# Transposing the normalised tiles by a DMA on ScalarE's queue instead of by TensorE, in the middle tiles of a hybrid decoder layer

## What is computed

```python
def rmsnorm(x, g):
    y = x32 * rsqrt(mean(x32 * x32) + EPS) * g
...
p = einsum('btd,dc->btc', rmsnorm(x, norm1), w_in)       # u | q | k | v | o | gates
x = x + mixer_output(pool_mix(u), mlstm(q, k, v, gates), o)   # ends in @ w_out
a = square(relu(rmsnorm(x, norm2) @ w_up))
x = x + a @ w_down
y = rmsnorm(x, norm_f)
```

## Time and profile before

| | |
|---|---|
| median of 3 runs | 804.48 us (803.3 to 806.3) |
| profiled execution | 802.35 us, span of its slowest core 801.2 us |
| spans of the eight cores | 791.9 to 801.2 us |
| busy, share of the span | TensorE 95%, VectorE 54%, ScalarE 45%, GpSimd 20% |

### The profile page before, as it was taken

How to read it: one execution, slowest core, us unless ns; L and a number is a source line. 1 busy time by engine, 2 the same in 40 slices (tenths; PEclk the granted TensorE clock), 3 DMA queues, 4 the chain that set the end, 5 groups by cost and what they waited for, 6 DMA issues and landing times.

```text
span 801.2 us, 16676 instructions; the slowest of 8 cores (791.9 to 801.2 us)
## 1 busy us (share of the span) xinstructions
PE 761.0 (95%) x6707; PEld 532.0 (66%) x6707; DVE 432.9 (54%) x955; ACT 364.3 (45%) x871; POOL 160.9 (20%) x243
## 2 busy tenths in 40 slices
PE   2799899989999999999999899999999999999996
PEld 1678677858787789788789687878544444444443
DVE  1755886766886957786847765422233342421212
ACT  4465685854777564777664664422110010101102
POOL 7622430433303330202220300100011111100000
PEclk9789999999999999999999999999999999999999
DMA  8999995243444341334121989891666455453511
GB/s 151 202 184 179 185 188 112 72 94 81 53 108 124 82 107 54 67 105 107 54 81 60 158 189 244 173 220 62 203 214 241 176 217 215 148 193 124 180 54 53
DMA packets 35860, 110.43 MB, mean 138 GB/s; under 512 B 3431, under 2 KB 6871, under 8 KB 31798
## 3 DMA queue, kind: packets, MB, share of 16 engines
q1 hardware_dynamic: 21150, 63.31, 26.0%
q0 software_dynamic: 9648, 29.20, 22.7%
q10 hardware_dynamic: 4984, 16.86, 5.5%
HBM read 96.41 MB, written 39.64 MB: 170 GB/s over the span
## 4 chain that ended last, share of the span: by engine, by line
PE 81%; DVE 9%; DMA 5%; ACT 2%; issue 1%; POOL 1%; DVEq 0%; ACTq 0%; POOLq 0%; SPq 0%
PE B L428 79%; DMA wk<-w_in 2%; PE B L431 2%; DVE zt L437 2%; DMA aTd<-ast 1%; DMA C0b<-sC 1%; DVE ast L434 1%; DVE xt L434 1%; DVE mixh L437 1%; DVE rows L441 0%; DVE cols L434 0%; DVE rows L684 0%; POOL Wa L448 0%; ACT Dt L425 0%; DVE wsm L441 0%
## 5 line engine op out<-in xcount | busy, mean ns | idle before, releaser
L428 PE MATMUL B<-xn2T,wup 128*128 128x256 bf16 (+1 forms) x2304 | 248.7, 265 | 1.8 <-ACT rr L425 1.5
L428 PEld LDWEIGHTS B<-xn2T,wup 128*128 128x128 bf16 x2304 | 204.4, 98 | 27.7 <-ACT rr L425 2.0
L428 PE MATMUL B<-wdn,aTl 128*128 128x512 bf16 (+1 forms) x952 | 211.4, 379 | 0.0
L428 PEld LDWEIGHTS B<-wdn,aTl 128*128 128x128 bf16 (+1 forms) x952 | 93.1, 99 | 110.0
L434 DVE TENSOR_TENSOR xt<-xt,B 128x512 f32<-128x512 f32 (+1 forms) x68 | 46.5, 684 | 170.7 <-PE B L428 170.6
L434 DVE TENSOR_TENSOR ast<-rr 128x512 bf16<-128x512 f32 x132 | 95.6, 725 | 76.6 <-ACT rr L425 47.7
L425 ACT ACTIVATE rr<-B 128x512 f32<-128x512 f32 x132 | 78.1, 592 | 88.6 <-PE B L428 72.2
L425 ACT ACTIVATE junk<-xt 128x1024 bf16<-128x1024 f32 (+2 forms) x18 | 18.2, 1010 | 203.2 <-DVE xt L434 203.2
L428 PE MATMUL B<-w_out_sb,mixT 128*128 128x512 bf16 (+1 forms) x272 | 62.8, 379 | 0.0
L425 ACT ACTIVATE xn<-xt 128x1024 bf16<-128x1024 f32 (+2 forms) x34 | 35.7, 1050 | 33.6 <-DVE xt L434 23.3
L448 POOL TENSOR_TENSOR kz<-ktm,wsm 64x512 bf16<-64x512 bf16 x16 | 16.3, 1034 | 167.5 <-PE B L428 151.3
(11 more groups left out here) (202 smaller groups left out, 951.9 us busy)
## 6 DMA issues: line engine op xcount, KB each, us to landing
aTd<-ast SPq DMA_DIRECT2D x32, 512.0 KB, 4.7
aTl<-aTd SPq DMA_DIRECT2D x16, 1024.0 KB, 6.4
wup<-w_up POOLq DMA_DIRECT2D x8, 1024.0 KB, 38.4
x2d<-xt SPq DMA_DIRECT2D x16, 512.0 KB, 3.8
xt<-x2d SPq DMA_DIRECT2D x16, 512.0 KB, 3.4
yp<-xt ACTq DMA_DIRECT2D x15, 512.0 KB, 3.5
wdn<-w_down POOLq DMA_DIRECT2D x7, 1024.0 KB, 13.0
xt<-xp SPq DMA_DIRECT2D x12, 512.0 KB, 5.3
```

The costliest lines, as they stand in the source:

```text
L428: return lambda: nc.tensor.matmul(out, lhsT=lhsT, rhs=rhs, start=start, stop=stop)
```

## The change

In `pre` from tile 6 on, and in `tail` where `pos` is 6 to 14, `trT` is replaced by `XPOSE`: one transposing DMA, issued by ScalarE, that reads `xn` (128x1024, bfloat16, 256 KB) and writes `xnT` or the half of `xn2T` directly. The multiplication by the norm weights then reads and writes that tile in place in SBUF, where it used to read the PSUM bank. That is 11 tiles in `pre` and 9 in `tail`, so 20 times eight transposes leave TensorE. The planner is given 1.2 us of ScalarE for each such issue and 400,000 bytes for its transfer, and it makes a new order for all engines from there on.

```diff
--- before.py
+++ after.py
@@ -21,6 +21,7 @@
 UPV = 1800
 PRE, FRONT, MID, TAIL, POOLP, OGP = -50, -50, 30, -150, 40, 60
 NBC = 5
+TX0, TX1 = 6, 14
 LOG = None
 
 
@@ -277,7 +278,7 @@
                     hold[self.kinds[v]].add(v)
             if o.chan is not None:
                 q = 'sw' if o.eng == 'pool' else 'hw'
-                free[o.eng] = o.start + (1.0 if q == 'sw' else 0.3 if o.eng == 'act' else 0.4)
+                free[o.eng] = o.start + (1.0 if q == 'sw' else o.cost if o.cost > 1.0 else 0.3 if o.eng == 'act' else 0.4)
                 r = self.SW_RATE if q == 'sw' else self.HW_BUSY if band['sw'] > free[o.eng] + 1.0 else self.HW_RATE
                 b = max(free[o.eng] + 0.6, band[q]) + o.nbytes / r
                 if r == self.HW_BUSY:
@@ -430,6 +431,9 @@
         def tr(out, in_, identity):
             return lambda: nc.tensor.transpose(out=out, in_=in_, identity=identity)
 
+        def XPOSE(prio, out, in_, R, W, chan):
+            pl.add('act', [lambda: nc.scalar.dma_start_transpose(out=out, in_=in_)], R, W, 1.2, prio, chan, 400e3, 512)
+
         def vtt(out, in0, in1, op):
             return lambda: nc.vector.tensor_tensor(out=out, in0=in0, in1=in1, op=op)
 
@@ -847,9 +851,13 @@
             xk = 'xnT%d' % ix(pos); X = xnT[ix(pos)]
             xs_ = pos % NX
             norm(pr, xt[xs_][:], 'xt%d' % xs_, st[s2], 'st%d' % s2, 128)
-            T = trT(pr, 128)
-            V(pr, vtt(X[:], Bb[T].rearrange("p (k t) -> p k t", k=8), gcol1.unsqueeze(2).to_broadcast([128, 8, 128]), ALU.mult),
-              [bk(T), 'gvec'], [xk], 1.2)
+            if pos < TX0:
+                T = trT(pr, 128)
+                V(pr, vtt(X[:], Bb[T].rearrange("p (k t) -> p k t", k=8), gcol1.unsqueeze(2).to_broadcast([128, 8, 128]), ALU.mult),
+                  [bk(T), 'gvec'], [xk], 1.2)
+            else:
+                XPOSE(pr, X[:], xn[:], ['xn'], [xk], 'tx%d' % ix(pos))
+                V(pr, vtt(X[:], X[:], gcol1.unsqueeze(2).to_broadcast([128, 8, 128]), ALU.mult), [xk, 'gvec'], [xk], 1.2)
 
         def front(pos):
             i = pos - 1
@@ -1014,11 +1022,16 @@
             DMA(pr, 'sp', x2d[128 * i:128 * i + n, :], x_[r_, :], [xk], ['x2d%d' % i], 'x2s%d' % xs_, 512e3)
             sk = 'st%d' % (2 + pos % 2)
             norm(pr, x_[r_, :], xk, st[2 + pos % 2], sk, n)
-            T = trT(pr, n)
             gs, half = (0, 0) if sp_ else ((i // 2) % 2, i % 2)
             xnk = 'xn2T%d%d' % (gs, half)
-            V(pr, vtt(xn2T[gs][:, :, half * 128:half * 128 + n], Bb[T].rearrange("p (k t) -> p k t", k=8)[:, :, r_],
-                      gcol2.unsqueeze(2).to_broadcast([128, 8, n]), ALU.mult), [bk(T), 'gvec'], [xnk], 1.2)
+            X2 = xn2T[gs][:, :, half * 128:half * 128 + n]
+            gB = gcol2.unsqueeze(2).to_broadcast([128, 8, n])
+            if sp_ or not TX0 <= pos <= TX1:
+                T = trT(pr, n)
+                V(pr, vtt(X2, Bb[T].rearrange("p (k t) -> p k t", k=8)[:, :, r_], gB, ALU.mult), [bk(T), 'gvec'], [xnk], 1.2)
+            else:
+                XPOSE(pr, X2, xn[:], ['xn'], [xnk], 'ty%d%d' % (gs, half))
+                V(pr, vtt(X2, X2, gB, ALU.mult), [xnk, 'gvec'], [xnk], 1.2)
 
         for gs in range(2):
             for half in range(2):
```

## The result

The changed kernel takes 806.38 us (median of 20 runs) against 803.89 us for the kernel before on the same chip. The ratio is **1.0039, 95% interval 1.0021 to 1.0057**. It is slower by 0.4%, where 0.8% faster was forecast: the time lies inside the range that was given, on the wrong side of the kernel before.

The account below looks back on a forecast made before the run. TensorE's work was taken to bound the kernel, without gaps in tiles 6 to 16. 802.35 - 9.0 + 2.5 = 795.9 us, plus 2.1 to the median: 798.0 us, 0.8% faster; range 793.5 to 814 us.

Parts of the forecast that it names:

- What leaves TensorE: Tiles 6 to 16: twenty groups of eight transposes at 0.45 us leave TensorE, all on the path, -9.0 us.
- What VectorE gains or loses: Norm-weight multiplication: 1.22 us from PSUM, taken as 1.22 again from SBUF, so 0 us.
- What the issue costs ScalarE: Twenty DMA issues at up to 1.36 us each, covered by ScalarE's idle time and a second bank: 0 us.
- the sign of being wrong that the prediction named: On ScalarE's queue: the forecast is wrong if issues of the transposing DMA are over 2.3 us.
- the first rival: ScalarE eats the gain: 0.3 to 0.5 us behind each of 20 issues, 800.5 to 808 us, chance 0.2.
- What the landing costs: Next norm and multiplication wait for DMAs landing in 5.2 us: 0.5 us at five places, +2.5 us.
- the 15 us that the prediction named: Wrong if ScalarE's waits for `xn`, or VectorE's for `xnT` and `xn2T`, add up to over 15 us.
- the second rival: Late landings stop ScalarE at the next norm in fourteen places; 817 us at 7.9 us landings, chance 0.18.
- the third: Each DMA transposes its blocks one after another, landing far over every cover: 877 us, chance 0.04.
- What comes late at the end: Last `w_down` load before `up` ends: cover shrinks from 25 us to some 16, so 0 us.

Follow-up runs that it names:

- e8: The changed kernel's order on every engine, with the 20 transposing DMAs issued by SyncE instead of ScalarE: 803.8 us, 1.0012 of the kernel before.
- the two moves: Changed kernel, first `down` matmuls put back before the second sixteen, GpSimd's third `w_down` load and the `kz` behind it moved behind the pooling: 802.7 us, 0.9994.
- e12: The changed kernel's plan without the 20 DMAs, their transposes left out of the computation, with the two moves: 796.1 us, 0.9918 of the kernel before.
- e11: The kernel before's plan, with ScalarE-issued transposing DMAs only in eight first-norm tiles with 5 us or more of cover: 807.7 us, 1.0066.
- e13: The kernel before's plan, with transposing DMAs in the same eight tiles as e11, issued by SyncE: 803.7 us, 1.0014.
- e6: The changed kernel's order with the 20 DMAs taken out and the transposes left out of the computation: 800.9 us, 0.9981 of the kernel before.
- e1: The kernel before in its own order, with seven of eight transposes left out in the 20 groups: 797.5 us, 0.9942.
- e3: Changed kernel, first `down` matmuls put back before the second sixteen, first `w_down` load waiting for the last transposing DMA's landing: 808.1 us, 1.0071.

## Why the prediction was wrong

The runs form a table. The step between the lower two rows holds the issue on ScalarE and the longer landings that went with it (see e8):

| ratio to before | new plan as made | with the two moves |
|---|---|---|
| no transfer | 0.9981 | 0.9918 |
| DMA issued by SyncE | 1.0012 | 0.9945 |
| DMA issued by ScalarE | 1.0039 | 0.9994 |

- **"What leaves TensorE", -9.0 us.** The mechanism was right, and the size can't be told from the measured one: 7.5 us of work left by the changed kernel's profile, 7.9 to 10.9 by the eight others with the same matmuls. In the mended plan without a transfer most of it arrives (e12, 0.8% or 6.6 us).
- **"What VectorE gains or loses", 0.** Right: 1.22 us from PSUM and 1.22 us in place, as medians.
- **"What the issue costs ScalarE", 0.** Wrong. In the median an issue is 1.23 to 1.30 us, below the 1.36 assumed, but the 1.36 was taken for an upper bound, and 57 of 160 were over it; the six over 2.3 us are the sign of being wrong that the prediction named. The step weighed it against a ReLU that TensorE can wait for 2.3 us, but behind an issue also stand `numS`, `mixh`, `interB`, which have no such reserve, and while the issue runs ScalarE does nothing else. Price by the table's columns 0.3 and 0.5%, by e11 against e13 0.5% for only eight: 2 to 4 us. The columns' price includes the longer landings of ScalarE's queue; that of e11 against e13 is nearly the issue alone. This is the first rival, which I gave 0.2, and 806.4 lies in its 800.5 to 808; but it put all of the loss here, and the last term weighs as much again. The estimate of 1.7 us an issue from the Trainium skill's "DMA: Bandwidth & Descriptors" is above the median here (1.23 to 1.30) and within the spread (up to 3.25).
- **"What the landing costs", +2.5.** About right in size: SyncE's issues against no transfer are 0.3% in both columns, about 2.3 us, what they do to SyncE's own transfers included. Where it falls was wrong. On ScalarE's queue it isn't spread over five places, but sits in the DMAs issued near 205 us (VectorE waits 1.2 to 4.2 us on six of eight cores) and near 440 us (1.1 to 2.6 us on four cores, the four slowest). On core 1 of the changed kernel one landing beside an `aTd` store and an `xt` load took 9.8 us; VectorE's timeline, then TensorE's:

```profile
215.12 1.42 DVE L438 TENSOR_TENSOR xn2T<-xn2T,gvec 128x1024 bf16<-128x1024 bf16 x1 [2.87 <-DMA xn2T<-xn]
...
218.50 0.25 PE L432 MATMUL B<-ident_f,R 68*128 68x68 f32 x1 [2.10 <-DVE zt L441]
```

  Behind the multiplication stand `rows` and `zt`, and TensorE waits for them. ScalarE waited at the next norm for 0.2 us at the most and VectorE for all landings together 6.7 us at the most by core, well below the 15 us that the prediction named; the stores around them landed about as before (medians: `aTd` 4.3 us, 4.7 before; `x2d` 3.9, 3.8 before). So the second rival fell, and so did the third: 128x1024 lands in 3.0 to 3.1 us at the best, by core. The Trainium skill's 1309 ns for a block ("VectorE: DVE Perf Modes", "The three transpose paths") doesn't add up over blocks here.
- **"What comes late at the end", 0.** Wrong, and the largest. I looked only at the last load of `w_down` and its 16 us of cover. What came late was the first use of `aTl`, pulled ahead by the planner (TensorE waits for it on all eight cores of the changed kernel, 0.8 to 5.0 us), and, near 455 us, what stands behind VectorE. That second wait has two sources, and the later one shows: on the slowest core the last landing, and without a transfer the pooling of the last tile behind a load that waits on GpSimd's queue (e6). Price of the two moves 0.45 to 0.7% in the three rows, 3.6 to 5.4 us, the lower clock behind each wait included. `up` ended at 574 us on core 3, not at the 557 forecast and later than the 565 of before.

By the left column: -1.5 us (plan without a transfer) + 2.5 (landing) + 2.2 (issue) = +3.2 us against +3.1 measured; these are steps of one column and meet the total by construction. Not settled: whether the move on GpSimd's queue would help the kernel before as well, where the same load stands in the same place with 0.7 us of the chain. No run has it, so a part of the 0.5% may be an improvement of its own and not a price of the new plan; e12 below e1 would fit that. Nor is it shown why e11 and e13 have only 0.4 and 1.7 us less work than before for 64 transposes fewer, though 3 us is about what the account can resolve.

## What to carry to other kernels

A change that makes a greedy planner plan anew is two changes. Take the added operation out of the new order and time that: here it showed 0.4 of the 1.0% between e1 and the changed kernel in one run, at a place that the change doesn't touch. Look in the new order for waits *on a queue*: an instruction that waits for a transfer in front of small operations of a dependent chain (GpSimd's third load, worth 0.5%) can cost as much as the whole transfer. A DMA isn't free for the engine that issues it: count what stands behind the issue, not the engine's idle share, and give it to a queue with nothing urgent behind it. And transposes through PSUM are also a buffer; a DMA that writes the target directly gives up that slack (24 us in the place above; no run prices it by itself).

## What the hardware showed that I had not expected

- A transposing DMA of 128x1024 in bfloat16 takes its queue at least 1.23 us to issue on ScalarE and 1.22 on SyncE, against 0.48 or 0.63 us for a plain one of the same bytes. Beside other traffic it took up to 3.25 us, and ScalarE did nothing in that time ("idle 3.37, issue").
- Its landing depends on company: 3.0 us at the least, 9.8 beside an `aTd` store and an `xt` load (core 1), up to 11.6 (core 6). With the first load of `w_down` held back (e3) the last one took 4.7 to 5.6 us instead of 5.1 to 10.0. The plain copy's longest on the profile's core was 6.8.
- On SyncE's queue, with stores and loads behind them, the same issues and landings together cost 0.3% against no transfer (both columns of the table); on ScalarE's 0.6 to 0.8%.
- Behind waits the granted clock falls. It was 1.00 (2.4 GHz) in the windows from 200 to 450 us and 0.92 from 450 to 515 us, where TensorE had waited 3.3 and 3.5 us; right behind these waits it was 0.50, the 1.2 GHz level, from 457.4 to 460 us, and 0.56 from 504 to 507 us. TensorE's timeline right behind the second wait:

```profile
503.95 5.30 PE L429 MATMUL B<-wdn,aTl 128*128 128x512 bf16 x16 [3.50 <-DMA aTl<-aTd]
```

  The same sixteen matmuls in the kernel before, without a wait ahead of them:

```profile
526.39 3.62 PE L428 MATMUL B<-wdn,aTl 128*128 128x512 bf16 x16
```
